# A two-layer streaming encoder step: forget-gate sums as columns, the sample's four heads in one attention unit, the short convolution moved into the first input product

## What is computed

```python
def ab_mixer(h, conv_prev, s0, past_k, past_v, past_logf, w_in, conv_w, ...):
    qkv_a, z_a, b_a, a_a, q_b, k_b, v_b, f_b = jnp.split(h @ w_in, idx, axis=-1)
    qkv_a, conv_new = causal_conv_silu(qkv_a, conv_prev, conv_w)      # 4 taps, then silu
    ...
    oa, s_new = gated_delta_rule(qa, ka, va, g, beta, s0)             # 4 heads
    oa = rmsnorm(oa, onorm_g) * silu(z_a)
    logf = log_sigmoid(f_b + f_bias)
    # the sample has 512 keys, values and logf of the past ahead of its own 32
    ob = fox_attention(q_b, k_all, v_all, lf_all)                     # 4 heads of 128
    return concatenate([oa, ob]) @ w_out, ...

def fox_attention(q, k, v, logf):
    F = cumsum(logf)                      # over the keys, for each head
    s = q @ k.T * D ** -0.5 + Fq[:, None] - F[None, :]
    s = where(kpos <= qpos, s, -inf)
    return softmax(s) @ v
```

## Time and profile before

| | us |
|---|---|
| median of 3 runs (lowest, highest) | 1752.03 (1749.71, 1754.26) |
| the profiled execution, its own time | 1760.79 |
| its span, first to last instruction | 1759.0 |
| PE busy | 1667.0 (95% of the span) |
| DVE busy | 765.3 (44%) |
| ACT busy | 607.2 (35%) |
| POOL busy | 531.3 (30%) |
| mean granted TensorE clock | 0.966 |

### The profile page before, as it was taken

How to read it: one execution, slowest core, us unless ns; L and a number is a source line. 1 busy time by engine, 2 the same in 40 slices (tenths; PEclk the granted TensorE clock), 3 DMA queues, 4 the chain that set the end, 5 groups by cost and what they waited for, 6 DMA issues and landing times.

```text
span 1759.0 us, 31567 instructions
## 1 busy us (share of the span) xinstructions
PE 1667.0 (95%) x13326; PEld 1568.5 (89%) x13326; DVE 765.3 (44%) x1403; ACT 607.2 (35%) x1120; POOL 531.3 (30%) x187
## 2 busy tenths in 40 slices
PE   6999888999988999999999999989889999999998
PEld 6999756888887899999999997559878999999998
DVE  4119753443574632222223623784746322223235
ACT  4113373221443442222223314783434323222232
POOL 4533300210252133443433432002621443433441
PEclk9999998899999999999999998899999999999999
DMA  5232300000433023223222223001320223222221
GB/s 150 74 95 76 119 26 1 8 2 13 144 114 103 25 72 97 82 87 96 89 78 95 73 96 133 1 1 49 120 97 25 80 89 97 90 78 95 81 86 51
DMA packets 123034, 131.39 MB, mean 75 GB/s; under 512 B 6285, under 2 KB 115122, under 8 KB 122930
## 3 DMA queue, kind: packets, MB, share of 16 engines
q1 hardware_dynamic: 116064, 123.27, 21.5%
q10 hardware_dynamic: 6866, 6.63, 1.2%
HBM read 122.44 MB, written 7.45 MB: 74 GB/s over the span
## 4 chain that ended last, share of the span: by engine, by line
PE 84%; DVE 10%; ACT 3%; issue 2%; DMA 0%; ACTq 0%; DVEq 0%
PE LP L722 66%; PE MP L839 3%; PE LP L1044 3%; PE LP L805 3%; PE MP L823 2%; DVE acc L1790 1%; DVE sq L2014 1%; PE LP L957 1%; DVE sq L2012 1%; DVE xl L1797 1%; PE MP L1138 1%; DVE probs L1856 1%; PE MP L1124 1%; PE MP L1132 0%; DMA stage<-in_w_in_ab 0%
## 5 line engine op out<-in xcount | busy, mean ns | idle before, releaser
L619 POOL TENSOR_TENSOR wl<-stage,wh 128x2048 fp32r<-128x2048 f32 x107 | 493.5, 4612 | 1017.5 <-ACT wh L1294 1017.4
L722 PE MATMUL LP<-xh,wh 128*128 128x272 f32 x2176 | 458.3, 292 | 14.3 <-DVE xl L1797 7.2
L722 PE MATMUL LP<-xh,wl 128*128 128x272 f32 x2176 | 452.9, 290 | 0.0
L722 PE MATMUL LP<-xl,wh 128*128 128x272 f32 x2176 | 452.3, 290 | 0.0
L1294 ACT CAST wh<-stage 128x2048 fp32r<-128x2048 f32 x107 | 203.7, 1904 | 462.7 <-PE LP L722 461.9
L722 PEld LDWEIGHTS LP<-xh,wh 128*128 128x128 f32 x2176 | 345.6, 190 | 19.3 <-DVE xl L1797 9.7
L722 PEld LDWEIGHTS LP<-xl,wh 128*128 128x128 f32 x2176 | 345.7, 191 | 0.0
L722 PEld LDWEIGHTS LP<-xh,wl 128*128 128x128 f32 x2176 | 342.9, 190 | 0.0
L722 PE MATMUL LP<-hh,wh 128*128 128x272 f32 x1024 | 211.2, 287 | 0.0
L722 PE MATMUL LP<-hh,wl 128*128 128x272 f32 x1024 | 210.6, 288 | 0.0
L722 PE MATMUL LP<-hl,wh 128*128 128x272 f32 x1024 | 210.3, 287 | 0.0
(11 more groups left out here) (357 smaller groups left out, 1877.7 us busy)
## 6 DMA issues: line engine op xcount, KB each, us to landing
stage<-in_w_up SPq DMA_DIRECT2D x32, 1024.0 KB, 5.3
stage<-in_w_down SPq DMA_DIRECT2D x32, 1024.0 KB, 5.2
stage<-in_w_in_ab SPq DMA_DIRECT2D x13, 1024.0 KB, 5.2
stage<-in_w_xkv SPq DMA_DIRECT2D x8, 1024.0 KB, 5.4
stage<-in_w_in_c SPq DMA_DIRECT2D x6, 1024.0 KB, 5.0
stage<-in_w_out_ab SPq DMA_DIRECT2D x4, 1024.0 KB, 7.1
stage<-in_w_xq SPq DMA_DIRECT2D x4, 1024.0 KB, 5.6
stage<-in_w_xo SPq DMA_DIRECT2D x4, 1024.0 KB, 5.9
```

Of the source, the lines that this page charges most:

```text
L619: pool.tensor_tensor(wl[s][:, :], stage[s][:, :], wh[s][:, :].bitcast(f32), ALU.subtract).then_inc(w_lo, 1)
L722: mm = pe.matmul(LP[:, 2 * slot + half, 0:b - a], weights, X[part][:, k, a:b], start=(first and n_ == 0), stop=(last and n_ == 2), skip_gr ...
```

## The change

Three things move, and the buffers follow them.

The convolution: DVE convolves row T - 4 right behind the drain of tile T of `in_a`, in four instructions over prompt and sample together (547 columns, into `conv_sum`), and ACT applies silu there. The silu of `z` and the load of the exp and ln table come after the twelfth row and ahead of the gates' arithmetic. In `in_b` DVE only drains.

The forget gates: PE makes the cumulative sums as columns, keys on partitions and heads on columns, with 13 small matmuls between the two panels of the first pair of `in_b`. ACT copies them to `forget`. Between the panels of the second pair, 16 matmuls with a column of `forget` spread as the stationary side and the identity as the moving side make the rows of the prompt in MP. The rows of the sample are made behind the first scores of the attention, 32 partitions for each head, and DVE adds the causal mask to them once.

The attention: one group of 17 units. The third is the sample, its four heads of 32 queries stacked on the 128 partitions.

The past keys take the place of `stage`, so they are loaded once the last panel of `in_b` has been split, and the first two panels of `out0` are loaded behind the attention and split within the delta rule. The diff, cut:

```diff
-        group("fox_p", fox_units(False))
-        group("fox_s", fox_units(True))
+        group("fox", fox_units())      # sample unit inserted at index 2
...
@@ SP
-            first_pair("out0")
-
-            sp.wait_ge(product_done, LIN["out0"][1])
             for dst, src_, signal in ((kp_rows, ...), (vp_n, ...)):
+                if dst is kp_rows:
+                    sp.wait_ge(w_lo, LIN["out0"][0])
+                else:
+                    sp.wait_ge(product_done, LIN["out0"][1])
                 sp.dma_start(...)
+            sp.wait_ge(ol_ready, sum(GROUP["fox"]))
+            first_pair("out0")
...
@@ PE
+            def forget_sums():
+                pe.wait_ge(gate_dve, GATE_LOGF)
+                pe.wait_ge(gate_in, 16 * 3)
+                for i, logf in enumerate((gates_raw[:, 0:TT, 2 * H:3 * H], lf_past[:, :, :])):
+                    out = MP[:, 0, TT * H * i:TT * H * (i + 1)].rearrange("p (j h) -> p j h", h=H)
+                    pe.matmul(out, upper[:, 0:128], logf, start=(i == 0), stop=False, ...)
+                    for j in range(TT - 1):
+                        pe.matmul(out[:, j + 1:TT, :], ones[:, :], logf[:, j:j + 1, :].to_broadcast(...), ...)
+                out = MP[0:NS, 0, 2 * TT * H:2 * TT * H + H]
+                for c in range(PAST // 128):
+                    pe.matmul(out, ones[:, 0:NS], lf_past[:, c, :], start=False, stop=False, ...)
+                pe.matmul(out, upper[0:NS, 0:NS], gates_raw[0:NS, TT, 2 * H:3 * H], ...).then_inc(forget_pe, 1)
+            one_pair("in_b", 0, XS, between=forget_sums)
...
+            def forget_rows():
+                pe.wait_ge(forget_act, 1)
...
+                for h in range(H):
+                    for j in range(TT):
+                        mm = pe.matmul(MP[:, h, 128 * j:128 * j + 128],
+                                       forget[:, H * j + h:H * j + h + 1].to_broadcast([128, 128]), ident[:, :], ...)
+                    mm.then_inc(rows_pe, 1)
+            one_pair("in_b", 1, XS, between=forget_rows)
+            pe.wait_ge(rows_act, H)
...
-            forget_rows(False)
...
+            def forget_rows_sample():
+                for c in range(PAST // 128):
+                    for h in range(H):
+                        past = forget[:, H * (TT + c) + h:H * (TT + c) + h + 1].to_broadcast([128, NS])
+                        pe.matmul(LP[NS * h:NS * h + NS, 2, 128 * c:128 * c + 128], past, ident[:, :], ...)
+                for h in range(H):
+                    mm = pe.matmul(LP[NS * h:NS * h + NS, 3, 0:NS], own, ident[0:NS, 0:NS], ...)
+                mm.then_inc(rows_pe, 1)
             def delta_sums(i):
+                if i == -1:
+                    forget_rows_sample()
+                if i == 0:
+                    pe.wait_ge(rows_act, H + 1)
+                    pe.wait_ge(turn_act, 2 * NTOK + PAST // 128)
...
-            forget_rows(True)
-            pe.wait_ge(rows_act, 2 * H)
-            attention("fox_s")
...
@@ PE, values of a stacked unit
+                        for g in range(U["stack"]):
+                            for c, (n, v) in enumerate(U["v"]):
+                                mm = pe.matmul(MP[:, 2 + u % 2, g * w:g * w + w], v[g], U["PT"][0:n, u % 2, at:at + w], ...)
...
@@ ACT
+            for T in range(NCONV + H):
+                if T % 2:
+                    split_after("in_a", T)
+                if T > CONV_LAG:
+                    conv_row(T - CONV_LAG - 1)
+            conv_row(NCONV - 1)
+            act.wait_ge(drained, DRAINED["in_b"])
+            act.activation(z[:, :, :], z[:, :, :], ACT.Silu).then_inc(conv_act, 1)
+            act.preload_act_table_set("natural_log_exp_and_others")
             act.wait_ge(gate_pe, 2)
...
             for what in DELTA:
+                if what in (("rec", "ws", 2, 0), ("rec", "ws", 2, 1)):
+                    split(what[3], 16 * (LIN["out0"][0] // 2 + 1))
...
@@ DVE
+            def conv_rows_sum(f):
+                if f >= 2:
+                    dve.wait_ge(conv_act, f - 1)
+                out, width = conv_sum[:, f % 2, :], UPAD - PAD
+                dve.tensor_scalar(out, ua[:, f, 0:width], conv_w(0, f), None, ALU.mult).then_inc(conv_dve, 1)
+                for i in range(1, CW):
+                    dve.wait_ge(conv_dve, CW * f + i)
+                    dve.scalar_tensor_tensor(out=out, in0=ua[:, f, i:i + width], scalar=conv_w(i, f), in1=out, ...)
...
+                if T >= CONV_LAG:
+                    conv_rows_sum(T - CONV_LAG)
```

More of the change, by code:

```diff
@@ L183, in build_program @@
         head_squares = place("head_squares", [128, 2, N], at=peak[0])
+        k_out = [place(f"k_out{j}", [128, H * HD], at=acc_at + 4 * H * HD * j if j < 3 else peak[0]) for j in range(TT)]
+        assert 3 * H * HD <= 3 * N
+        forget = place("forget", [128, 2 * TT * H + H], at=peak[0] + 4 * H * HD)
         gates_start = peak[0] + 4 * 2 * N
@@ L341, in unit, with fox_units @@
         def unit(**kw):
-            kw["G"], kw["nk"] = len(kw["q"]), sum(n for _, n in kw["keys"][0])
+            kw.setdefault("stack", 1)
+            kw["G"], kw["nk"] = len(kw["q"]) // kw["stack"], sum(n for _, n in kw["keys"][0])
             return kw
-        def fox_units(sample):
+        def fox_units():
             out = []
@@ L801, in scores @@
                         pe.wait_ge(ex_ready if UNITS[u - 2]["kind"] == "cross" else nm_ready, u - 1)
-                    for g in range(U["G"]):
-                        at = g * U["nk"]
-                        for kT, n in U["keys"][g]:
-                            mm = pe.matmul(LP[0:U["P"], 2 * (u % 2) + at // 512, at % 512:at % 512 + n], U["q"][g],
+                    for g, keys in enumerate(U["keys"]):
+                        stacked = U["stack"] > 1
+                        rows, at = (slice(NS * g, NS * g + NS), 0) if stacked else (slice(0, U["P"]), g * U["nk"])
+                        for kT, n in keys:
+                            mm = pe.matmul(LP[rows, score_bank(u, at // 512), at % 512:at % 512 + n], U["q"][g],
                                            kT, start=True, stop=True, skip_group_check=True)
@@ L1447, in _ @@
             store(t["o_s_fox_logf"][0, 0], gates_raw[0:NS, TT, 2 * H:3 * H])
[L1449 to L1451 removed]
             for T in range(NCONV):
[L1453 removed]
+                if T % 2 and T < NCONV - 3:
                     split_after("in_b", T)
+                if T == 2:
+                    act.wait_ge(forget_pe, 1)
+                    n_ = 2 * TT * H
+                    act.activation(forget[:, 0:n_], MP[:, 0, 0:n_], ACT.Copy, scale=-1.0)
+                    act.activation(forget[0:NS, n_:n_ + H], MP[0:NS, 0, n_:n_ + H], ACT.Copy, scale=-1.0
+                                   ).then_inc(forget_act, 1)
+                if T == 6:
+                    for h in range(H):
+                        act.wait_ge(rows_pe, h + 1)
+                        act.copy(nF[:, h, 0:NPT], MP[:, h, :]).then_inc(rows_act, 1)
                 if T == 7:
                     for j, a, P in TOK:
[L1457 removed]
+                        row = k_out[j][:, :] if j < TT else k_out_s[:, :]
                         act.wait_ge(turn_pe, j + 1)
```

246 lines of the change are left out of this document (121 added, 125 removed).

## The result

The changed kernel takes 1736.72 us (median of 12 executions, 1728.5 to 1747.93), the kernel before 1757.94 beside it (12 executions); the ratio is 0.9881, 95% interval 0.9849 to 0.9912. That is about 21 us faster, where 38 were forecast, and 1736.7 lies outside the range of 1703 to 1727. The profiled execution after has a span of 1739.3 us and an own time of 1740.99.

What follows compares the result with a forecast made beforehand. PE was taken to bound the kernel, with 98.7 us between `in_b` and the gate sums as target. `in_b` +6.0, first scores -19.0, attention 43.1 to 52.5, sample stretches gone (16.6, 18.1): -38.1, 1752.0 to 1714; range 1703 to 1727.

Steps and rivals of the forecast that it cites:

- Step 1: First input product `in_a`: DVE keeps up with the added convolution despite POOL holding it; costs 0, upper end 2 us.
- Step 2: Start of `in_b`: gates come later, at 142.4, and PE waits 2.3 us for them (0 to 6.8).
- Step 3: Forget sums in `in_b`: 13 small matmuls take 3.1 us, then two slow-clock tiles add 2.2 us.
- Step 4: Prompt's forget rows in `in_b`: 16 matmuls of 128 columns take 3.8 us (1.9 to 7.4).
- Step 5: k and v transposes in `in_b` lose stalls: -2.5, -2.2 and -0.7 us; `in_b` sums to +6.0, ends at 217.9.
- Step 6: From `in_b` to first scores: the 20.9 us stretch shrinks to 1.91 us of key transposes; -19.0, scores at 219.8.
- Step 7: Attention of 17 units: rows' wait +2.3, serial scores +3.8, transposes and values +3.3; 52.5 us, ending at 272.3.
- Step 8: Sample's forget rows (16.6 us) and attention (18.1) go; gate sums start at 272.5, -38.1 us, nothing due earlier afterwards.
- (c): Rival: the whole attention falls to the low clock after a pause near its start; +23 us, 1737, chance 0.07.
- (d): Rival: convolution bounds `in_a`, slower; one lock per tile 1742, chance 0.04; two locks 1796, chance 0.02.
- a lock on every tile: Rival case in `in_a`: POOL holds DVE once each tile, 8.3 us per tile, 28 us lost, 1742; chance 0.04.

Runs made afterwards that it cites:

- the single band: Kernel with 30 added waits, the first head's sample score computed four more times into one 32-row band, against that kernel; 1716.68 us, one execution.
- the loop at 236: Changed kernel with 30 satisfied waits added at the start of TensorE's program, layer-0 MLP loop starting at 236 modulo 256; 1717.76 us, ratio 0.9777 to the kernel before.
- at 255: Changed kernel with 49 satisfied waits added at the start of TensorE's program, layer-0 MLP loop starting at 255 modulo 256; 1730.32 us, ratio 0.9854.
- modulo 206 in layer 1: Changed kernel with 56 satisfied waits added at the start of TensorE's program, layer-1 MLP loop starting at 206 modulo 256; 1732.45 us.

## Why the prediction was wrong

**Step 1**, right. `in_a` ends within 0.1 us of before, one DVE instruction for each panel is held by POOL. The row ahead of the gates ended at 135.8 (forecast near 135.2).

**Step 2**, right: gates at 142.8 (142.4), wait 2.56 us (2.3).

**Step 3**, right in kind: the slow tiles took 14.66 us where 14.2 was forecast. The sums were priced at the full clock, 3.1, while the clock had fallen already behind the wait: 4.3. (At the full clock they take 2.3.) That the wait is what brings the clock down is not shown: with the convolution back it fell without a wait, behind the sums, and the tiles took 13.75.

**Step 4**, right: 3.57 us (3.8).

**Step 5**, the sum right, the cause wrong. The stalls shrank as said (k wait from 3.21 to 0.75 us, the slow tiles behind it from 14.28 to 12.03), and `in_b` ended at 218.94 (217.9, 1.0 us too little). But the prediction put this down to the convolution's leaving, and with the convolution back the wait is 0.75 us just the same. What differs from before there as well is that the sums and the rows put TensorE 8.6 us later at the k transposes (184.91 against 176.31), which gives ScalarE the time it lacked; that this suffices is argued.

**Step 6**, right: first scores at 220.52 (219.8).

**Step 7**, right in its sum, by two errors. The scores took 1.09 and the 32-wide ends 0.27, side by side, not 3.8: "each band's 512-wide matmul is followed by its own 32-wide one, so I take the serial value" chose the wrong end of its own two, and the single band with 3.61 us shows what the other would have been. The estimate of 1.2 to 1.6 that the prediction drew from the Trainium skill (TensorE: Matmul & The Clock Gate, Part 3: Packing small matmuls) and set aside came near: the Trainium skill has 2.38 times for three bands, here four bands were 3.3 times faster than one (3.61 / 1.09). Against that, the values took 6.2 us, not 4.8: 1.24 to 1.35 for each of the first three heads and 2.26 for the last, at a granted clock of 0.55. The wait for the sample's rows was 2.78 (2.3), from the cause it named. Attention and gate sums: 272.02 (272.5).

**Step 8**, the first half right: the gate sums start 38.6 us earlier (38.1; the steps as written add up to 38.3). The sentence that failed is "From there on nothing is due earlier than before". It looked at transfers and engines and found nothing to lose, and it did not ask what a shorter TensorE program does to code that stands behind it. It moved the layer-0 MLP loop by 49 instructions onto one of 28 bad places in 256, for 16.1 us, where the prediction had nothing; the medians miss 16.9 of the 38.1. With the loop at 236 the gain is 39 us in the medians (1756.53 to 1717.76), ratio 0.9777, where the forecast is 0.9783; at 255 it is 28 (1758.41 to 1730.32), for which the window attention is the likely but unproven reason. The other 4.1 us of the profiled execution lie in the window attention and are not the change's.

**The rivals.** None was it. The nearest time, (c), 1737, had another mechanism: the attention's clock was 0.94. (d) had a point for it, VectorE held by POOL, and did not come about; its case of a lock on every tile was priced at 1742, still below the 1752 of before and so not "slower". The range failed since it held only mechanisms in the stretch that was edited. With what the runs show now, a loop of this length has a chance of 28 in 256, some 11%, to start on a bad place; the prediction had no such term.

## What to carry to other kernels

An edit that adds or drops instructions moves every loop behind it in the program. For a long loop, count its instructions and where it starts, before comparing two versions: here, by the count of pieces, one place in nine costs some 8 us at each jump back, more than many changes bring. The sign in the profile is idle time of TensorE ended by "issue" at the top of a pass, with more packets on its instruction queue than before; some satisfied waits at the program's idle start, or writing the loop out, cured it here. And when the lead of a change is lost, compare the start of a regular event, like the low part of each weight panel, between the two traces: the cause lies where the difference jumps, or as far ahead of it as the event lags (here two panels at most).

## What the runs showed of the hardware

- TensorE's jump back over 1564 instructions cost nothing in the kernels where they lie in 7 pieces of 256 by P's count, and 5.7 to 9.1 us where they lie in 8: 4.0 to 5.7 us of standstill, the rest the low clock behind it. (At modulo 206 in layer 1 one of two jumps was free.)
- Straight code, fetched at one packet of 256 instructions every 16 us (12 in 192 us), ran without a pause beside transfers of 88 GB/s in the mean.
- 66 satisfied waits left TensorE's first transpose at 9.8 us, 207 put it at 23.63. With one price for each wait that is at least (23.63 - 9.79) / 141 = 98 ns, and at most 23.63 / 207 = 114 ns. The delay divided by 207, 66 ns, is too little, since the first waits pass in idle time.
- Four products of 512 columns in four 32-wide bands ran in 1.09 us, four such products in one band in 3.61.
- A pause of 2.56 us ahead of small products was followed by the low clock for these and for part of the next two tiles (14.66 us for 12.04); nearly the same products without the pause left it at 1.00 in one kernel, and in another were followed by 0.50 from 145 to 147 us and 13.75 us for the two tiles.
